# Two stacked blocks in one kernel: passages of the second block rebuilt, with two norms from one pass of sums, the context half behind the residual half, and branch parts in the last slots

## The reference, cut to what matters

```python
    h = h + gate * (p[i] @ w_ple[i])
return rmsnorm(h, norm_final)
# second block, x = that result, ctx = context of 256 tokens
for l in range(2):
    shift, scale, gate = jnp.split((silu_c @ w_mod[l] + b_mod[l])[:, None, :], 3, axis=-1)
    h  = modulate(x, g_pre[l], shift, scale)        # rms_norm(x, g) * (1 + scale) + shift
    hc = modulate(ctx, g_pre[l], shift_c, scale_c)
    # one wide projection of h, and of hc (last layer: of hc the rk, rv, dk, dv columns alone)
    # retention, differential attention (its keys and values: context and x), gated chunk MLP
    out = merge_branches(o_ret, o_mlp, o_diff, mlog, w_branch_out[l], w_out[l])
    x = x + gate * rms_norm(out, g_post[l])         # ctx likewise, after layer 0
```

## Time and profile before

| | |
|---|---|
| median of 3 runs | 1717.1 us (1715.94 to 1718.62) |
| the profiled execution | 1714.67 us, its span 1712.9 us |
| mean granted clock of TensorE | 0.957 of full speed |
| TensorE matmul busy | 1555.7 us, 91% |
| VectorE, ACT, POOL busy | 55%, 43%, 7% |
| the chain that ended last, by engine | TensorE 80%, VectorE 8%, ACT 6%, DMA 4% |
| HBM read | 220.94 MB, 130 GB/s over the span |

### The profile page before, as it was taken

How to read it: one execution, slowest core, us unless ns; L and a number is a source line. 1 busy time by engine, 2 the same in 40 slices (tenths; PEclk the granted TensorE clock), 3 DMA queues, 4 the chain that set the end, 5 groups by cost and what they waited for, 6 DMA issues and landing times.

```text
span 1712.9 us, 25830 instructions
## 1 busy us (share of the span) xinstructions
PE 1555.7 (91%) x9958; PEld 1360.4 (79%) x9958; DVE 939.0 (55%) x1481; ACT 729.8 (43%) x1245; POOL 121.5 (7%) x145
## 2 busy tenths in 40 slices
PE   6999998889999889868898898999997998988996
PEld 6999997679999867656677777888774887878996
DVE  5777776537777568565533335233326446435554
ACT  5444562554444454225433253222325355435443
POOL 3700000130000130001000000000000011010000
PEclk9999998999999999989999999999998999989999
DMA  8655543246777433431111122333320332314662
GB/s 288 213 184 182 179 161 107 92 144 227 241 236 246 161 123 123 148 123 37 37 62 62 50 74 74 99 111 111 110 75 25 119 106 71 111 51 146 202 205 99
DMA packets 72662, 223.22 MB, mean 130 GB/s; under 512 B 6656, under 2 KB 23552, under 8 KB 71936
## 3 DMA queue, kind: packets, MB, share of 16 engines
q1 hardware_dynamic: 54528, 195.20, 34.7%
q10 hardware_dynamic: 18048, 26.82, 4.8%
HBM read 220.94 MB, written 1.05 MB: 130 GB/s over the span
## 4 chain that ended last, share of the span: by engine, by line
PE 80%; DVE 8%; ACT 6%; DMA 4%; issue 2%; POOL 0%; SPq 0%; DVEq 0%; ACTq 0%
PE ps L476 68%; DMA ring<-stream 3%; PE ps L486 2%; DVE w_lo L415 1%; PE ps L891 1%; ACT w_hi L1084 1%; ACT area L1333 1%; PE ps L932 1%; PE ps L949 1%; PE ps L875 1%; DVE area L2094 1%; PE ps L912 1%; DVE area L1914 1%; DVE area L1523 1%; PE ps L831 1%
## 5 line engine op out<-in xcount | busy, mean ns | idle before, releaser
L476 PE MATMUL ps<-hn_hi,w_hi 128*128 128x256 f32 (+1 forms) x1888 | 616.4, 326 | 59.8 <-DVE w_lo L415 33.9
L476 PE MATMUL ps<-hn_lo,w_hi 128*128 128x256 f32 (+1 forms) x1888 | 605.9, 321 | 0.0
L476 PE MATMUL ps<-hn_hi,w_lo 128*128 128x256 f32 (+1 forms) x1888 | 605.4, 321 | 0.0
L415 DVE TENSOR_TENSOR w_lo<-ring,w_hi 128x1024 fp32r<-128x1024 f32 (+1 forms) x331 | 395.5, 1200 | 359.5 <-ACT w_hi L1084 355.4
L1084 ACT ACTIVATE w_hi<-ring 128x1024 fp32r<-128x1024 f32 (+1 forms) x347 | 359.6, 1037 | 350.8 <-DMA ring<-stream 241.9
L476 PEld LDWEIGHTS ps<-hn_hi,w_hi 128*128 128x128 f32 x1888 | 366.6, 194 | 93.0 <-DVE w_lo L415 37.0
L476 PEld LDWEIGHTS ps<-hn_lo,w_hi 128*128 128x128 f32 x1888 | 366.7, 194 | 24.2
L476 PEld LDWEIGHTS ps<-hn_hi,w_lo 128*128 128x128 f32 x1888 | 365.9, 194 | 24.9
L1147 ACT ACTIVATE area<-ps 128x512 f32<-128x512 f32 (+1 forms) x164 | 80.8, 503 | 348.1 <-PE ps L476 337.0
L476 PE MATMUL ps<-area_r,w_hi 128*128 128x256 f32 (+1 forms) x512 | 117.7, 324 | 2.0 <-DVE w_lo L415 1.9
L476 PE MATMUL ps<-hid_hi,w_hi 128*128 128x256 f32 x352 | 99.4, 282 | 2.4 <-DVE w_lo L415 1.2
(11 more groups left out here) (295 smaller groups left out, 1665.1 us busy)
## 6 DMA issues: line engine op xcount, KB each, us to landing
ring<-stream SPq DMA_DIRECT2D x359, 512.0 KB, 3.6
mod_at<-mod_stream ACTq DMA_DIRECT2D x29, 512.0 KB, 5.4
area<-mod_stream ACTq DMA_DIRECT2D x17, 512.0 KB, 4.1
pk<-pack ACTq DMA_DIRECT2D x1, 1610.0 KB, 7.0
pk<-pack SPq DMA_DIRECT2D x1, 1549.0 KB, 12.4
h<-x_in SPq DMA_DIRECT2D x1, 1024.0 KB, 5.0
cond_at<-cond SPq DMA_DIRECT2D x2, 512.0 KB, 14.4
mod_at<-mod_stream SPq DMA_DIRECT2D x2, 512.0 KB, 12.6
```

The source lines that it names most:

```text
L415: eng.tensor_tensor(lo[:, 0:w], raw, hi[:, 0:w].bitcast(F32), ALU.subtract).then_inc(lo_ready[who], 1)
L476: m = pe.matmul(dst, w_, x_, start=(start and n == 0), stop=(stop and n == 2), skip_group_check=True)
```

## The change

Of the modulations ten are made in the first FFN (steps `EARLY_AT`) and twelve late, in three slots, each load issued by ACT at a weight's high part. Into the second block, the context's squares are summed ahead of "plew" and its modulated half is made before the gates are evicted; squares of h and of g*h go side by side, and the final norm's root and the first pre-norm's root come from one pass of sums: the mean square after the final norm is mean((g h)^2) times the squared first root. `final_norm` itself is written later. Layer 1 starts with dq and rq, that need x alone, while the context is added to, summed and modulated; dk follows, and the ropes have another order. Squared sums of "wo" go between its units, squares are taken from PSUM. Two branches get their parts in the slots after the last retention step, and the mv norms overlap. The diff, cut, with leading indentation taken off:

```diff
 MODS = LAYERS * 3 * KT
-EARLY_MODS = 5
+EARLY_AT = [0, 1, 2, 3, 4, 8, 11, 14, 17, 20]
...
+HEAD_PARTS = [("dk", "dq", "dv", "dg"), ("dq", "rq", "dk", "dv", "dg")]
+SLOT_PARTS = [("rk", "rq", "rv", "rg", "mv", "mu", "mg"), ("rk", "rv", "rg", "mv", "mu", "mg")]
+ROPE_ORDER = [("dk", "dq", "rk", "rq"), ("dq", "rq", "dk", "rk")]
...
+first = 16 if l == 0 else 12
 for step in range(len(RET[l]) + 2):
-    slots[16 + step].append(("ret", step))
+    slots[first + step].append(("ret", step))
+for n, b in enumerate((0, 2)):
+    slots[first + len(RET[l]) + 2 + n].append(("branch", b))
...
-late_mod_slot = lambda m: as_mod(retz[:, 8 + 2 * (m % 2):10 + 2 * (m % 2), :])
+late_mod_slot = lambda m: as_mod(retz[:, 6 + 2 * (m % 3):8 + 2 * (m % 3), :])
...
+def load_late_mod(eng, m):
+    if m >= LATE_MOD + 3:
+        eng.wait_ge(s("mod_used"), m - 2)
+    eng.dma_start(late_mod_slot(m), mod_stream[m]).then_inc(s(f"late_loaded{m % 3}"), 16)
...
+sumsq(4)
...
 for j in range(2, KT):
     project(("pleg", j))
-sumsq(4, T)
...
+    if j >= 3:
+        sumsq(5, 2 * T, tiles=[j - 3])
+sumsq(5, 2 * T, tiles=range(KT - 3, KT))
...
+def project2(name, l, tokens, ctx_by_tile=False):
+    wt = split_unit(name)
...
+if ctx_by_tile:
+    pe.wait_ge(s("ctx_modulated"), KT * l + k + 1)
...
-project_pair([("dk", l, 0), ("dk", l, 1)], 2 * T, s("modulated"), [16 * l + 2 * k + 2 for k in range(KT)])
...
+pe.wait_ge(s("ctx_modulated"), KT)
+project_pair([("dk", l, 0), ("dk", l, 1)], 2 * T, s("modulated"), [k + 1 for k in range(KT)])
...
+else:
+    sumsq(7)
+    project_pair([("dq", l, 0), ("dq", l, 1)], T, s("modulated"), [KT + k + 1 for k in range(KT)])
+    for j in (2, 3):
+        project2(("dq", l, j), l, T)
+    for j in range(4):
+        project2(("rq", l, j), l, T)
+        if j == 1:
+            sumsq(8, T, T, 6)
+    project2(("dk", l, 0), l, 2 * T, True)
+    rotate4("dq", l)
+    project2(("dk", l, 1), l, 2 * T)
+    project2(("dk", l, 2), l, 2 * T)
+    rotate4("rq", l)
+    project2(("dk", l, 3), l, 2 * T)
 for cc_ in range(4):
...
+if l == 1 and cc_ == 1:
+    rotate4("dk", l)
...
-sumsq(6 + 2 * l, tok)
+    sumsq(6 + 3 * l, tok, tiles=[j - 2])
+sumsq(6 + 3 * l, tok, tiles=(KT - 2, KT - 1))
...
+late = u - UNIT["dk", 0, 3] + LATE_MOD
+if LATE_MOD + 3 <= late < MODS:
+    load_late_mod(act, late)
...
-if f < EARLY_MODS:
-    load_mod(act, m0 + f + 1)
...
+if n == 0:
...
+if f <= 4:
+    load_mod(act, f + 1)
+elif f % 3 == 0:
+    load_mod(act, f // 3 + 4)
+part(3 * f + 4)
...
+act.wait_ge(block2_loaded, 32)
+for k in range(KT):
+    act.activation(sq[:, k, T:2 * T], hc[:, k, :], ACT.Square).then_inc(squares_ready, 1)
...
 hn_high(3)
-for j in range(KT):
-    take(("pleg", j), plg[:, j, :], ACT.Sigmoid)
-root_table()
...
-load_mod(act, LATE_MOD)
-load_mod(act, LATE_MOD + 1)
-late = [LATE_MOD + 2]
-def next_mod(l):
-    if l == 0 and late[0] < MODS:
-        load_mod(act, late[0])
-        late[0] += 1
+root(3, bank(6, 0, T), T, sumsq_ready, 4, D, s("ctx_rstd"), T)
+def modulated_high(l, st):
+    for k in range(KT):
+        act.wait_ge(scaled_ready[st], KT * l + k + 1)
+        v = slice(T * st, T * st + T)
+        act.activation(hn[0][:, k, v], sq2[:, k, v], ACT.Identity, bias=mods[:, l, k, st:st + 1])\
...
+modulated_high(0, 1)
+for j in range(KT + 2):
+    if j < KT:
+        take(("pleg", j), plg[:, j, :], ACT.Sigmoid)
+    if j == KT - 1:
+        root_table()
+    if j >= 2:
+        k = j - 2
+        act.wait_ge(resid_ready, 8 + k + 1)
+        act.activation(sq[:, k, 0:T], h[:, k, :], ACT.Square)
+        act.activation(sq[:, k, T:2 * T], h[:, k, :], ACT.Square, scale=c("g_final", k, k + 1)).then_inc(squares_ready, 1)
+act.wait_ge(sumsq_ready, 6)
+link(act.activation(lnr[:, 0:T], bank(7, 0, T), ACT.Ln, bias=eps[:, 0:1], scale=1.0 / D))
+act.activation(aux[:, 8, 0:T], lnr[:, 0:T], ACT.Exp, scale=-1.0).then_inc(s("final_square"), 1)
+act.activation(rstd[:, 0:T], lnr[:, 0:T], ACT.Exp, scale=-0.5).then_inc(rstd_ready, 1)
+act.wait_ge(rstd_ready, 5)
+act.wait_ge(s("final_mean"), 1)
+link(act.activation(lnr[:, 0:T], aux[:, 8, T:2 * T], ACT.Ln, bias=eps[:, 0:1], scale=1.0 / D))
+act.activation(aux[:, 9, 0:T], lnr[:, 0:T], ACT.Exp, scale=-0.5).then_inc(s("x_rstd"), 1)
+for m in range(LATE_MOD, LATE_MOD + 3):
+    load_late_mod(act, m)
...
-for k in range(KT):
-    if l == 1:
-        act.wait_ge(resid_ready, RESID_BLOCK2 + k + 1)
-        act.wait_ge(s("ctx_ready"), k + 1)
-    else:
-        act.wait_ge(resid_ready, RESID_BLOCK2 - KT + k + 1)
-    act.activation(sq2[:, k, 0:T], h[:, k, :], ACT.Square)
-    act.activation(sq2[:, k, T:2 * T], hc[:, k, :], ACT.Square).then_inc(squares_ready, 1)
-root(0, bank(7), 2 * T, sumsq_ready, 6 + 2 * l, D, rstd_ready)
...
-    act.wait_ge(s("cond_kept"), 2)
-for k in range(KT):
-    for st in range(2):
-        act.wait_ge(scaled_ready, 16 * l + 2 * k + st + 1)
-        v = slice(T * st, T * st + T)
-        act.activation(hn[0][:, k, v], sq2[:, k, v], ACT.Identity, bias=mods[:, l, k, st:st + 1])\
-            .then_inc(s("hn_high2"), 1)
-    if k == 3:
-        prepare(("dk", l, 0))
+    modulated_high(0, 0)
+    prepare(("dk", l, 0))
...
-t_ = 2 * T if part == "dk" else tok
-take((part, l, j), diffz[:, (0 if part == "dk" else 4) + j, 0:t_], tokens=t_)
-if (part, j) > ("dk", 1):
...
+    take_part("dk", range(4))
+    take_part("dq", range(4))
+else:
+    prepare(("dq", l, 0))
+    for k in range(KT):
+        act.wait_ge(resid_ready, RESID_BLOCK2 + k + 1)
+        act.activation(sq2[:, k, 0:T], h[:, k, :], ACT.Square).then_inc(squares_ready, 1)
+    root(7, bank(7, 0, T), T, sumsq_ready, 8, D, s("x_rstd"))
+    modulated_high(1, 0)
+    def ctx_squares(tiles):
+        for k in tiles:
+            act.wait_ge(s("ctx_ready"), k + 1)
+            act.activation(sq2[:, k, T:2 * T], hc[:, k, :], ACT.Square).then_inc(squares_ready, 1)
+    take_part("dq", (0, 1))
+    ctx_squares(range(4))
+    take_part("dq", (2, 3))
+    ctx_squares(range(4, KT))
+    take_part("rq", (0, 1))
+    prepare(("rq", l, 2))
+    root(8, bank(6, 0, T), T, sumsq_ready, 9, D, s("ctx_rstd"), T)
+    modulated_high(1, 1)
+    take_part("rq", (2, 3))
+    take_part("dk", range(4))
...
-    next_mod(l)
 for j in range(4):
...
+        branch_high(l, step)
 if part == "mv" and j == 3:
...
-for n, b in enumerate((0, 2, 1)):
+for n in range(3):
     prepare(("mlog", l, n, 0))
-    for g in range(4):
-        act.wait_ge(s("mixed"), 4 * l + (g + 1 if b == 1 else 1))
-        act.activation(branch_hi[b][:, g, 0:tok], branches[b][:, g, 0:tok], ACT.Copy).then_inc(s("branch_high"), 1)
+branch_high(l, 1)
...
-    take(("wo", l, j), unnormed[:, j, 0:tok], tokens=tok)
-for k in range(KT):
-    wait_taken(act, ("wo", l, k))
-    act.activation(sq2[:, k, 0:tok], unnormed[:, k, 0:tok], ACT.Square).then_inc(squares_ready, 1)
-root(0, bank(7, 0, tok), tok, sumsq_ready, 7 + 2 * l, D, rstd_ready)
+    prepare(("wo", l, j))
+    product(act, "wo", l, j)
+    o = bank(BANK["wo", l, j][0], 0, tok)
+    act.activation(sq2[:, j, 0:tok], o, ACT.Square).then_inc(squares_ready, 1)
+    act.activation(unnormed[:, j, 0:tok], o, ACT.Copy).then_inc(act_evac, 1)
+root(6, bank(7, 0, T), T, sumsq_ready, 7 + 3 * l, D, s("out_rstd"))
+if l == 0:
+    root(6, bank(7, T, T), T, None, 0, D, s("out_rstd"), T)
...
-if f < EARLY_MODS:
-    modulation(f)
...
+if 5 <= f < 7:
+    turn_tables(f - 5)
...
+if f in EARLY_AT:
+    modulation(EARLY_AT.index(f))
...
+for k in range(KT + 1):
+    if k < KT:
+        stt(sq2[:, k, v], x[:, k, :], gain(k), r, ALU.mult, ALU.mult).then_inc(scaled_ready[st], 1)
+    if k >= 1:
+        dve.wait_ge(high, KT * l + k)
+        stt(hn[1][:, k - 1, v], sq2[:, k - 1, v], mods[:, l, k - 1, st:st + 1],
+            hn[0][:, k - 1, v].bitcast(F32), ALU.add, ALU.subtract).then_inc(ready, 1)
+    if k in lows:
+        low_until(lows[k])
...
+v = slice(T * st, T * st + T)
+for k in range(tiles[0], tiles[0] + len(tiles) + 1):
+    if k in tiles:
+        stt(unnormed[:, k, v], unnormed[:, k, v], pgate[:, l, k, st:st + 1], rstd[:, v], ALU.mult, ALU.mult)\
+            .then_inc(s(f"out_scaled{st}"), 1)
+    if k - 1 in tiles:
+        dve.wait_ge(s(f"out_scaled{st}"), KT * l + k)
+        tt_(x[:, k - 1, :], x[:, k - 1, :], unnormed[:, k - 1, v], ALU.add).then_inc(done, 1)
...
+dve.wait_ge(mods_ready, 3)
+tt_(gamp[:, :], amp[:, 0, :, 0], c("g_final"), ALU.mult).then_inc(mods_ready, 1)
+dve.wait_ge(s("ctx_rstd"), 1)
+modulated(0, 1, hc, lambda k: amp[:, 0, k, 1:2], rstd[:, T:2 * T])
 for j in range(KT):
     wait_taken(dve, ("pleg", j))
     link(tt_(plg[:, j, :], plg[:, j, :], pwp[:, j, :], ALU.mult))
     tt_(h[:, j, :], h[:, j, :], plg[:, j, :], ALU.add).then_inc(resid_ready, 1)
...
-final_norm()
...
+low_until(("dk", 0, 1))
...
+dve.wait_ge(s("x_rstd"), 1)
+dve.wait_ge(rstd_ready, 5)
+link(tt_(aux[:, 9, T:2 * T], aux[:, 9, 0:T], rstd[:, 0:T], ALU.mult))
...
+tok = 2 * T if l == 0 else T
+for g in range(4):
```

(76 more changed lines are left out.)

196 lines of the change are left out of this document (98 added, 98 removed).

## The result

| | before | after |
|---|---|---|
| median | 1717.8 us (1715.94 to 1718.62, 4 runs) | 1698.05 us (1697.39 to 1698.63, 4 runs) |
| ratio | | 0.9886, 95% interval 0.9869 to 0.9903 |
| span of the profiled execution | 1712.9 us | 1695.8 us |
| mean granted clock | 0.957 | 0.962 |

1699.6 was forecast. The sum of the terms was -17.5 us against the profiled execution; its span fell by 17.1. Whether the terms are right is a question for the stages.

The account below looks back on a forecast made before the run. TensorE, busy 91% of the span, was taken as the bound, so time falls only where it waits or runs at low clock. Terms summed to -17.5 us: 1697.2 from the profiled execution, 1699.6 from the median; range 1688 to 1710.

Parts of the forecast that it names:

- 1 moved modulations: First FFN: five moved modulations ahead of w2 low parts cost 0.3 us each, +1.5 us.
- 2 into the second block: Passage into the second block: context high parts hold gate unit 2, the tail gets shorter; +3.5 us in all.
- 3 late modulations: Second block, layer 0: TensorE's waits of 6.24 and 11.22 us go with their clock falls, -22.3 us.
- 4 branch, layer 0: Branch parts of layer 0: the 4.97 us wait for mlog 2 goes with its clock fall, -7.4 us.
- 4 branch, layer 1: Branch parts of layer 1: mlog 2 no longer waits, the w_bo low part still does; -5.1 us.
- 5 between the layers: Between the layers: new waits at rq 0, rq 1, dk 0, dk 3, dv 2 and low clock, +14.6 us.
- 6 slots of layer 1: Slots of layer 1: rv 3's evictions +1.0 us, the pipelined layer norm of mv -2.0 us.
- 7 end: After the last product: two sums instead of eight and pipelined additions, -1.3 us.
- Rival C: First FFN: the moved modulations are exposed, 12.3 us instead of 1.5, giving 1710 us; chance 0.1.
- Rivals A, B and D: A: context half hides, 1677, chance 0.08; B: clock holds, 1690, 0.2; D: late modulations still hold low parts, 1721.9, 0.06.

Follow-up runs that it names:

- e1: The kernel after, with the five modulations moved into the first FFN made behind the next w2 unit's low part instead of ahead of it; 1686.8 us.
- e8: The kernel after, with the high and low parts of all three branches made behind the mixing products again in both layers; 1702.8 us.
- e4: The kernel after, with layer 1's low part of dk 0 made ahead of the modulated context half instead of behind it; 1692.8 us.
- e5: The kernel after, with layer 1's rq 0 cast ahead of the context squares and low parts of rq 0 and rq 1 ahead of context additions; 1699.7 us.
- e11: The kernel after with gate unit 2 cast ahead of the context root, context half one tile a gate, gate low parts on VectorE instead of POOL; 1687.1 us.
- e2: The kernel after, with gate unit 2 cast ahead of the context root and gate units 3 and 4 between the context high parts; 1690.9 us.
- e3: The kernel after, with layer 1's low part of dk 3 made ahead of rq's rope and that of dv 2 ahead of dk's; 1683.2 us.
- e10: The kernel after with e1, e3, e4, context half one tile a gate, gate unit 2 cast early, rq 0 cast and rq 1 low part earlier; 1663.56 us.
- e12: The kernel of e10 with the gate units' low parts made on VectorE instead of POOL; 1664.85 us, ratio 0.9701 to the kernel before.
- e6: The kernel after, with two slots for the late modulations instead of three, each load still issued at a weight's high part; 1697.3 us.

## Why the prediction was right, point by point

| term | forecast | measured | by |
|---|---|---|---|
| 1 moved modulations | +1.5 | +5.5 | A; +3.6 to +6.8 by the kernels with its code; e1 takes 4.3 of it off again |
| 2 into the second block | +3.5 | +2.1, and C -0.4 | D; last gate to first dk 10.1 (9.8 forecast) |
| 3 late modulations | -22.3 | -21.2 | E; from dq's rotation on -22.4 |
| 4 branch, layer 0 | -7.4 | -7.6 | G; e8 gives 7.4 back |
| 4 branch, layer 1 | -5.1 | -4.0 | J; -4.9 to -6.6 by the other kernels with its code; the wait left is 1.69 (1.7 forecast) |
| 5 between the layers | +14.6 | +11.8 | H less 13.0 of moved work |
| 6 slots of layer 1 | -1.0 | -0.5 | I plus 13.0 |
| 7 end | -1.3 | -0.4 | K |
| B and F, no term | 0 | -2.7 | |
| sum | -17.5 | -17.4 | span -17.1, the rest before the first product |

Each number is from one trace, and stages of the same code differ by up to 3.5 us; so a miss of 1 us says nothing. Right for the right reasons, then, in the four large terms: the two late waits and their falls, the gate unit held by the context half, the five new waits of layer 1 and their places, and the branch parts. The exact sum is partly luck: term 1 cost 4 us more than forecast and terms 3, 4, 6 and 7 gave 3.4 less; against them stand 2.8 in term 5, 1.8 in term 2 with C, and 2.7 in B and F.

**Term 1 failed as a size.** "I take 0.3 us for each of five" came from one step, where the low part had 2.15 us to spare. The steps that got a modulation had less, 1.3 at the one shown above (97.08 and a low part of 1.2, against 99.58), and the five waits are 0.7 to 1.65 us, 1.2 on the average beside the one of before. Rival C had the place right, and twice the price.

**Term 5** was close in its waits (13.9 us, 14.75 forecast). Most of the 2.8 us lies elsewhere: the six sums between the w_o products seem to cost 3.4 us (49.8 from the wait at w_o to the last product's end, against 46.35), and "the same work" had them at 5.3 (6 of 8 of the 7.13 in the earlier trace rows). But that price was about right: with the low clock that the kernel before had in this stretch (2.7 us of it), e1, e4, e5, e8 and e11 took 51.05 to 51.4 (2.8 to 3.1 us of it), 4.7 to 5.0 more than before. The trace of the kernel after had 1.45 us of it, and so some 1.5 of the 2.8 are luck. The handovers that I added (0.9) don't show. The Trainium skill ("TensorE: Matmul & The Clock Gate", section "HAM oscillation — how this bites in real kernels") has a kernel that stops TensorE between groups pay the cold start each time; by it dk 0 had to lose the full 2.4 us, against my half a fall. dk 0 took 7.33 us, and 5.64 in e4 without the wait: 1.7 lost, between my 1.2 and the 2.4 and a little nearer to the half.

Two small sums in the working are off: 646.9 less 643.68 is 3.2 and not 3.5 (part 2), and 4.42 less 1.7 is 2.7 and not 2.9 (part 4).

**One sign was wrong.** "It would be wrong if ... VectorE still waits for a late modulation's transfer": VectorE waits for six of them, 10.4 us in all, and TensorE loses nothing by it, because the low part ahead is already made. The sign should have been TensorE's wait alone.

**Rivals A, B and D** did not come about: the waits of layer 1 came, the falls behind them came, and no load held a low part that TensorE was waiting for.

## What to carry to other kernels

An in-order queue hides work only if what the bounding engine wants next is ahead of it: twelve us came from putting two low parts ahead of two ropes, five from one ahead of the context half, four from five modulations behind a low part. Before putting one ahead, look what its input waits for, and what now comes behind it; e5 put a cast ahead whose transfer had not landed, and the wait only moved to the next unit. And judge an edit by the stage it touches, and by how much that stage differs where nothing was changed: e2 made the run 7 us shorter and its own stage 0.2, e8 cost 10.8 us in its stages and 4.7 in the run.

## What was not expected of the hardware

What the low clock costs comes in pieces of one size. Summed over the whole span, idle stretches too, (1 - granted clock) times the length is 73.5 us before, 64.5 after, 60.0 in e3, 49.7 in e10 and 58.1 in e12, and in all fourteen traces each fall costs 1.7 us or 2, 3 or 4 times that, but for the last one, which the end of the span cuts off. I had priced a fall at 2.4, which is between one piece and two. How many pieces it is was not the same for equal waits: the first gate products follow an idle time of 2.75 us in every kernel, and

```profile
597.86:603.84 5.98, 5.98 (x48) 5.78 (x48) 4.56 (x15) 4.41 (x8) 1.32 (x1) 1.00 0.00 1
```

```profile
601.00:607.00 6.00, 5.63 (x26) 5.66 (x27) 5.89 (x19) 3.54 (x9) 0.00 (x0) 0.50 0.00 0
```

before they ran at 1.00 and after at 0.50. It takes no change of the kernel for that. e3 to e6 have the code of the kernel after up to this place and beyond, and in e6 the same products follow the same 2.75 us at 1.00:

```profile
603.91:609.89 5.98, 5.98 (x48) 5.77 (x48) 5.67 (x19) 3.57 (x9) 0.00 (x0) 1.00 0.00 0
```

The 48 matmuls of the first pair of gate units took 5.98 us in e6, 7.4 to 7.5 in e3, e4 and e5, and 8.67 in the kernel after. The falls thus differ from one execution to the next, and this is part of the spread: F took 264.6 to 265.0 us with 15.4 to 17.1 us of low clock, and 266.8 to 268.0 with 18.8 to 20.5. It is not all of it: A differs by 3.2 us with 1.7 us of low clock or less. What decides a fall, and what makes A differ, was not settled by these runs.

The other surprise is POOL: a low part of 2.4 us there made a VectorE step of 0.42 last 2.5. The prediction named this hold-up and, with one gate unit of slack, took it for nothing.
